# Odd modulation tiles scaled and accumulated by GpSimd, key reciprocals taken over 512 columns

## What is computed

```python
mod = c_act @ w_mod[l] + b_mod[l]                       # 2048 x 12288, one row of c
sh1, sc1, g1, sh2, sc2, g2 = split(mod, 6)
h = rms_norm(x, norm_attn[l]) * (1.0 + sc1) + sh1       # likewise with sc2, sh2 before the ffn
...
k = qk_norm_rope(concatenate([k_nope, k_rope], -1), k_norm_g, cos, sin)   # rmsnorm over 192
```

## Time and profile before

| | |
|---|---|
| three runs | 2112.49, 2118.07, 2120.44 us, median 2118.07 |
| the profiled execution | 2113.76 us, its span 2112.0 us |
| PE busy | 2075.8 us, 98% |
| DVE busy | 1577.2 us, 75% |
| ACT busy | 1008.3 us, 48% |
| POOL busy | 54.4 us, 3% |
| read from memory | 476 MB, 228 GB/s on average |

### The profile page before, as it was taken

The page is one execution under the profiler, slowest core; times in us unless marked ns, Lnnn a source line. Parts: engine busy times, 40 slices in busy tenths (PEclk is TensorE's granted clock), DMA queues, the critical chain, the costliest instruction groups (busy, mean ns, idle before and its releaser), DMA issues.

```text
span 2112.0 us, 41562 instructions
## 1 busy us (share of the span) xinstructions
PE 2075.8 (98%) x17878; PEld 2041.3 (97%) x17878; DVE 1577.2 (75%) x2034; ACT 1008.3 (48%) x1293; POOL 54.4 (3%) x87
## 2 busy tenths in 40 slices
PE   7999999999999999999999999999999999999999
PEld 7999999999999999989999888999999999999998
DVE  7998788688577888687877798676666666666666
ACT  5444343444445476564446555454444444444443
POOL 1000000000000000000002102000000000000000
PEclk9999999999999999999999999999999999999998
DMA  7897887789676687577796664456666666666663
GB/s 251 279 351 273 307 306 270 252 290 325 210 260 178 212 287 265 176 260 252 258 347 204 217 178 140 148 168 194 195 181 207 193 194 195 183 207 192 195 194 120
DMA packets 248430, 481.13 MB, mean 228 GB/s; under 512 B 28331, under 2 KB 57623, under 8 KB 248247
## 3 DMA queue, kind: packets, MB, share of 16 engines
q1 hardware_dynamic: 247487, 478.26, 69.7%
q0 software_dynamic: 528, 0.15, 0.0%
q10 hardware_dynamic: 232, 0.06, 0.0%
HBM read 476.27 MB, written 8.44 MB: 230 GB/s over the span
## 4 chain that ended last, share of the span: by engine, by line
PE 93%; DVE 3%; issue 1%; ACT 1%; DMA 1%; POOL 0%; SPq 0%; DVEq 0%; ACTq 0%
PE acc L1797 87%; PE side L1797 3%; PE sums L1797 2%; PE sums L2074 1%; DVE w_lo L1125 1%; DMA mod_raw<-in_w_mod 1%; DVE mod_acc L1113 1%; PE acc L1904 0%; ACT prob L978 0%; ACT w_hi L629 0%; DMA x_tok<-in_x 0%; DVE m_prob L1510 0%; DMA raw<-in_b_w_out 0%; POOL prob L609 0%; PE acc L2348 0%
## 5 line engine op out<-in xcount | busy, mean ns | idle before, releaser
L1125 DVE TENSOR_TENSOR w_lo<-raw,w_hi 128x1024 fp32r<-128x1024 f32 x679 | 831.0, 1232 | 428.2 <-ACT w_hi L629 427.2
L629 ACT ACTIVATE w_hi<-raw 128x1024 fp32r<-128x1024 f32 x679 | 716.8, 1060 | 845.3 <-PE acc L1797 758.5
L1797 PE MATMUL acc<-h_hi,w_hi 128*128 128x256 f32 x3728 | 885.3, 280 | 17.6 <-issue 11.8
L1797 PE MATMUL acc<-h_lo,w_hi 128*128 128x256 f32 x3728 | 876.0, 277 | 0.0
L1797 PEld LDWEIGHTS acc<-h_hi,w_hi 128*128 128x128 f32 x3728 | 703.3, 189 | 32.1 <-issue 23.4
L1797 PEld LDWEIGHTS acc<-h_lo,w_hi 128*128 128x128 f32 x3728 | 703.4, 189 | 0.3 <-issue 0.2
L1797 PE MATMUL acc<-h_hi,w_lo 128*128 128x256 f32 x3728 | 502.4, 277 | 0.0
L1797 PEld LDWEIGHTS acc<-h_hi,w_lo 128*128 128x128 f32 x3728 | 460.4, 188 | 0.0
L1113 DVE SCALAR_TENSOR_TENSOR mod_acc<-mod_raw,silu_c,mod_acc 128x1024 f32<-128x1024 f32 x180 | 230.9, 1283 | 11.2 <-DMA mod_raw<-in_w_mod 11.2
L1797 PE MATMUL acc<-f_hi,w_hi 128*128 128x256 f32 x704 | 164.3, 276 | 0.0
L1797 PE MATMUL acc<-f_lo,w_hi 128*128 128x256 f32 x704 | 164.1, 276 | 0.0
(11 more groups left out here) (320 smaller groups left out, 2041.8 us busy)
## 6 DMA issues: line engine op xcount, KB each, us to landing
mod_raw<-in_w_mod SPq DMA_DIRECT2D x192, 512.0 KB, 5.9
raw<-in_w_up SPq DMA_DIRECT2D x176, 512.0 KB, 4.4
raw<-in_a_w_in SPq DMA_DIRECT2D x128, 512.0 KB, 5.1
raw<-in_w_down SPq DMA_DIRECT2D x88, 512.0 KB, 4.4
raw<-in_a_w_out SPq DMA_DIRECT2D x64, 512.0 KB, 5.0
raw<-in_w_in SPq DMA_DIRECT2D x56, 512.0 KB, 4.1
raw<-in_b_w_in SPq DMA_DIRECT2D x40, 512.0 KB, 4.7
raw<-in_a_w_group SPq DMA_DIRECT2D x32, 512.0 KB, 5.4
```

The source lines that it names most:

```text
L629: last = act.activation(w_hi[s][:, :], raw[s][:, :], ACT.Copy)
L1125: last = dve.tensor_tensor(w_lo[s][:, :], raw[s][:, :], f32(w_hi[s][:, :]), ALU.subtract)
L1797: return pe.matmul(o, lhsT, rhs, start=start, stop=stop, skip_group_check=True)
```

## The change

- `mod_tiles` is written a second time for POOL: the odd tiles of the first five vectors (80 tiles) are scaled in place (`tensor_scalar`) and added into `mod_acc` (`tensor_tensor`), two instructions of 128x1024; DVE keeps the even ones and all of the sixth vector. `mod_used` becomes two semaphores. `MOD_PACE` runs from (306, 134) straight to (336, 160).
- The keys: PE multiplies ones by the squares themselves (512 columns, at the last slab of the gates), ACT takes the root over 512 columns, DVE the reciprocal over 512 columns. The four key columns on PE, `m_diag` and the copy are gone.
- The first slab behind a norm (`first_slab`) does high by high first, then low by high, then high by low, so that it starts with `h_hi` alone. DVE splits three of the slabs, and ACT two, inside the norm loop and not before it.
- DVE adds the two halves of the summed squares, so that `norm_sums` has two matmuls less.
- The products with `w_uk` and `w_uv` go to `sums` and `side` for their first halves; the second out-projection keeps two sets open over all eight slabs; `m_low(0, 2)` moves ahead of `m_soft` for the last pair; at the very end `turn_out(2)` moves into the last slab.

```diff
+GP_MODS = 5
-            (294, 128), (314, 148), (324, 148), (336, 160), (341, 160), (363, 176), (385, 186), (396, 192))
+            (294, 128), (306, 134), (336, 160), (341, 160), (363, 176), (385, 186), (396, 192))
                     if n >= MOD_RING:
-                        sp.wait_ge(mod_used, n + 1 - MOD_RING)
+                        sp.wait_ge(mod_used[(n - MOD_RING) % 2], (n - MOD_RING) // 2 + 1)
+            def mod_tiles(first, end):
+                for n in range(first + 1, end, 2):
+                    v, k = n // MOD_TILES, n % MOD_TILES // 2
+                    x, o = mod_raw[n % MOD_RING], mod_acc[:, 1024:2048]
+                    gp.wait_ge(mod_landed[n % MOD_RING], (n // MOD_RING + 1) * 16)
...
+                        gp.tensor_scalar(x[:, :], x[:, :], silu_c[:, k:k + 1], 1.0, ALU.mult, ALU.mult).then_inc(mod_scaled, 1)
+                        gp.wait_ge(mod_scaled, mod_steps.value())
+                        gp.wait_ge(mod_used[1], n // 2)
+                        gp.tensor_tensor(o, o, x[:, :], ALU.add).then_inc(mod_used[1], 1)
+            gp.wait_ge(csilu_ready, 1)
+            mod_tiles(0, 104)
             for m in range(1, 4):
                 gp.wait_ge(sq_ready, m + 1)
...
+            mod_tiles(104, GP_MODS * MOD_TILES)
-                act.wait_ge(m_recip, pairs.value())
-                for n in range(4):
-                    last = act.activation(m_diag[:, n * P:(n + 1) * P], tab("ident"), ACT.Copy, scale=m_rinv[:, n:n + 1])
-                last.then_inc(m_diag_ready, 1)
+            def m_key_roots():
+                act.wait_ge(m_spread, pairs.value())
+                act.activation(m_kroot[:, :], sums[:, 1, :], ACT.Sqrt, bias=eps_key[:, :]).then_inc(m_kroot_ready, 1)
+            def m_key_reciprocals():
+                dve.wait_ge(m_kroot_ready, pairs.value())
+                dve.reciprocal(m_kinv[:, :], m_kroot[:, :]).then_inc(m_kinv_ready, 1)
+                    if j % 2 and n < GP_MODS * MOD_TILES:
+                        continue
             def h_split(shift):
                 for j in range(KD // 2):
                     h_part(j, shift)
+                    if j < 2:
+                        split(1)
...
+            def first_slab(a, hi, lo, x_hi, x_lo, k, ready):
+                pe.wait_ge(h_hi_ready, ready + 1)
+                for x, (w, starts) in ((x_hi, (hi, True)), (x_hi, (lo, False)), (x_lo, (hi, False))):
...
+            def m_spreads(n):
+                if n:
+                    pe.wait_ge(m_turned_in, heads.value())
+                pe.wait_ge(m_folded, pairs.value())
+                mm(sums[:, 1, :], ones[:, 0:P], flat(tmp[0][:, 0:2, :]), start=True, stop=True).then_inc(m_spread, 1)
...
-            sets = [set_free()]
+            pe.wait_ge(att[0]["mix_hi"], TILES)
+            homes = [sums_tiles]
```

More of the change, by code:

```diff
@@ L1201, in norm @@
                     low(j)
+                    if j < 3:
+                        split(1)
                     if j + 2 < KD // 2:
@@ L1537, in _ @@
                 at, last = pair_at(n), n == PAIRS - 1
+                if last:
+                    m_low(0, 2)
                 if n:
@@ L1543, in _ @@
                     rope_keys()
-                if last:
-                    m_low(0, 2)
                 split_to(at + 7)
@@ L1823, in last_slab, with gemm @@
                         last.then_inc(tail_done, 1)
+                        if between:
+                            between()
                 last.then_inc(slab_used, 1)
                 slabs.step()
-            def gemm(n_slabs, x_hi, x_lo, tiles, k=SLAB_K, n=SLAB_N, before=None, x0=0, between=None, a=None, parts=None, tail=False):
+            def first_slab(a, hi, lo, x_hi, x_lo, k, ready):
+                pe.wait_ge(h_hi_ready, ready + 1)
+                for x, (w, starts) in ((x_hi, (hi, True)), (x_hi, (lo, False)), (x_lo, (hi, False))):
+                    if w is lo:
+                        pe.wait_ge(lo_ready, slabs.value(RING + 1))
+                    if x is x_lo:
+                        pe.wait_ge(h_lo_ready, ready + 1)
+                    for i in range(4):
+                        for kk in range(k):
+                            last = mm(a[:, i, :], w[:, kk, i * P:(i + 1) * P], x[:, kk, :], start=starts and i % 2 == 0 and kk == 0)
+                last.then_inc(slab_used, 1)
+                slabs.step()
+            def gemm(n_slabs, x_hi, x_lo, tiles, k=SLAB_K, n=SLAB_N, before=None, x0=0, between=None, a=None, parts=None, tail=False, first=None):
                 if a is None:
@@ L1834, in gemm @@
                     lo = w_lo[w][:, 0:k * n].rearrange("p (k n) -> p k n", k=k)
+                    if first is not None and s == 0:
+                        pe.wait_ge(hi_ready, slabs.value(1))
+                        first_slab(a, hi, lo, x_hi, x_lo, k, first)
+                        continue
                     if before:
@@ L1843, in gemm @@
                             x = s * k + kk + x0
-                            first = s == 0 and kk == 0 and i % 2 == 0
-                            mm(a[0:rows, i, :], hi[:, kk, c0:c0 + rows], x_hi[:, x, :], start=first)
+                            starts = s == 0 and kk == 0 and i % 2 == 0
+                            mm(a[0:rows, i, :], hi[:, kk, c0:c0 + rows], x_hi[:, x, :], start=starts)
                             mm(a[0:rows, i, :], hi[:, kk, c0:c0 + rows], x_lo[:, x, :])
@@ L1973, in _ @@
                 for m in range(2):
-                    gemm(8, h_hi, h_lo, four, before=h_ready(0))
+                    gemm(8, h_hi, h_lo, four, before=h_ready(0), first=0 if g == 0 and m == 0 else None)
                     if g == 0 and m == 0:
@@ L2263, in _ @@
             for m in range(3):
-                gemm(8, h_hi, h_lo, four, before=h_ready(24))
+                gemm(8, h_hi, h_lo, four, before=h_ready(24), first=24 if m == 0 else None)
             for m in range(2):
@@ L2284, in _ @@
                 slabs.step()
-            sets = [set_free()]
+            pe.wait_ge(idx_relu, TILES)
+            homes = [side]
             for r in range(2):
@@ L2325, in _, with ff_up @@
             ffs = Count()
-            def ff_up(before=None):
-                for m in range(2):
-                    gemm(8, h_hi, h_lo, four, before=before)
+            def ff_up(before=None, first=None):
+                gemm(8, h_hi, h_lo, four, before=before, first=first)
+                gemm(8, h_hi, h_lo, four, before=before)
             def ff_down(a):
```

204 lines of the change are left out of this document (101 added, 103 removed).

## The result

The changed kernel takes 2175.0 us, the median of four runs (2159.2 to 2191.0), against 2117.1 for the kernel before (2112.5 to 2120.4, four runs): a ratio of 1.027, 95% interval 1.023 to 1.031. It is slower, and outside the forecast range of 2095 to 2148. The profiled execution is one of 2191.0 us.

A forecast was written before the change was run, and what follows sets the result against it. PE, busy 98% of the span, was taken as the bound, DVE close behind. Losses of 32 us less gains of 24.6 made +7.4 on the profiled 2113.76, 2121; the runs' median being 4.3 higher, 2125, range 2095 to 2148.

The forecast's parts named there:

- The price of POOL's tiles: Odd modulation tiles on POOL: their turns slow DVE, PE waits; 26 of the 32 us of losses.
- The turns: A two-input SBUF instruction of DVE and a POOL instruction do not run side by side but take turns.
- The price of a tile: Each odd tile on POOL costs DVE 2.6 us against 1.2 saved, net 1.4; bounds of the cost 1.3 to 2.95.
- setting the net work of a stretch against its time: PE waits in a stretch only by what DVE's work exceeds its time and lead; 11 us in slabs 16 to 62.
- Key columns: Pairs: four key columns, eight matmul instructions, leave PE's path, 0.81 us for each of 8 pairs: 6.5 us gained.
- Start of the out-projection: PE's 3.51 us wait for m_low(0, 2) goes, and with it a clock dip worth 1.7: 5.2 us gained.
- Accumulator sets and norms: Waits for accumulator sets and xT go (3.3, 3.0, 1.2 us); the two norms gain 1.8.
- the fifth slab behind the norm: PE starts 2.8 us sooner, but the fifth slab's high part comes late, about 1052.0; 1.2 us of gain left.
- The end: Last chain: 8 token-square instructions go and 8 transposes move into the last slab; 2.5 us gained.
- The ports cost little: Rival, chance 0.32: POOL's instructions fall on DVE's waits, loss 6 us, gains of 24.6 stay; 2099 us.
- POOL is late and holds up SP: Rival, chance 0.26: SP waits for POOL's tile use, weight loads queue behind; 2147 us, or 2143 with part of it.
- P: DVE is blocked while POOL works; the forecast's losses from this were 32 us, between 6 and 54.

The follow-up runs named there:

- e1: The changed kernel without POOL's share, all modulation tiles back on DVE: 2135.4 us, ratio 1.001 to the kernel before.
- e6: e1 with the modulation tiles' pace of the kernel before: three runs at 2105.7 to 2113.5 us, seven at 2132 to 2141, ratio 1.004.
- e9: e6 with the norm ahead of the feed-forward part as in the kernel before: ratio 0.9945 to the kernel before.
- e3: The changed kernel with POOL's two instructions working in place on the accumulator's odd half, not the loaded tile: 2140.7, 2169.7, 2170.4, 2170.7 us.
- e5: e3 with SP's waits corrected so that SP no longer waits for POOL: 2139.7, 2141.0, 2164.4, 2167.5 us.

## Why the prediction was wrong, point by point

It gave 24.6 us of gains and 32 of losses, +7.4 on the profiled execution. Measured, with the wide spacing taken out: +44.6. Two terms failed, the price of POOL's tiles by 24 us and the gains by 14.

**The price of POOL's tiles, 26 forecast, 49.8 measured.** 26 is the sum of 32 less the 6 that I gave to the reciprocals and the denser pace. By stage, changed kernel against e1, from the start of ACT's high part of one slab to that of another, wide spacing taken out (the forecast's column holds those 6 too, in the last two rows):

| stage | forecast of the whole loss | measured, POOL's share |
|---|---|---|
| start to slab 66 | 11 | 10.7 |
| slabs 66 to 122 | 3 | 5.3 |
| slabs 122 to 192 | 1.5 | 2.9 |
| slabs 192 to 245 | 0 | 2.5 |
| pairs, slabs 245 to 289 | 5.5 | 19.3 |
| slab 289 to the in-projection | 11 | 9.0 |

*The turns* were read rightly from the earlier trace rows, and the Trainium skill's page "SBUF — State Buffer", section "Who interferes with whom", has them as the trace does: an instruction of DVE with two inputs in SBUF and one of POOL that reads SBUF exclude each other for a whole instruction. The trace agrees: the two `w_lo` shown above end 1.1 us after their additions. *The price of a tile was too high*: every DVE instruction of the changed kernel against the median of its form before adds up to 149 us too long, 6 of them in e1 too: 1.8 for each of the 80 odd tiles, not 2.6. With 1.28 saved the net is 0.5, and by DVE's busy time 46.7/80, 0.6, not 1.4. *The step that failed is the one after it*: setting the net work of a stretch against its time. With the measured 0.6 that sum gives 120.5 + 16 x 0.6 = 130.1 in slabs 16 to 62, which fits into 130.5, and yet 10.7 us were lost up to slab 66. That the forecast had 11 there is luck: a price too high made up for what the sum leaves out. In the pairs 13 us net and 17.5 of reciprocals against 150 gave 5.5; in slabs 134 to 188, 141.5 "fits into 147". Work comes in bursts: an addition of 2.4 us in front of a low part, then a tile, then the next low part. One such burst is longer than DVE's lead of 1.1, and PE, which is busy all the rest of the time, never makes a wait good. In the pairs the bursts also hit instructions that I hadn't put on the path:

```profile
847.61 2.39 POOL L617 TENSOR_TENSOR mod_acc<-mod_acc,mod_raw 128x1024 f32<-128x1024 f32 x1
847.71 2.83 DVE L1539 TENSOR_TENSOR m_prob<-m_prob,m_inv 128x512 f32<-128x512 f32 x1
850.60 0.88 PE L2123 MATMUL sums<-table,m_prob 128*128 128x128 f32 x6 [3.23 <-DVE m_prob L1539]
```

The scaling of the probabilities, 0.68 us when alone, took 2.83, and PE stood 3.23. *The clock was left out of the loss*, though I had counted it among the gains. Behind this wait comes a stretch at a granted clock of 0.50, and so it is behind some of the others, not all (none behind the 2.36 us until 116.20). There are 11 such stretches in the changed kernel and 6 in e1. At half speed they cost at most 31.0 and 18.4 us. By the pages PE is idle 70.9 us of the span against 38.5, so 32.4 of idle time and 12.6 of clock make 45.0 of the 49.8; the other 4.8 I can't place.

**The gains, 24.6 forecast, 5 measured in e1, 11 in e6.** The table's denser pace took 4 to 6 back, which the forecast had only as a part of its 32.

*Key columns, 6.5 forecast, 1.0 measured* (e6 against before, slabs 245 to 289). The term was right: where nothing waits, a pair takes 27.8 us (in e6, from PE's first matmul that reads `kq` at 760.2 to the next pair's at 788.0) where it took 28.6. But PE now waits for `kq L1520`, three times, 2.8 us, and for `m_prob` once. PE came sooner and DVE did not.

*Start of the out-projection, 5.2 forecast, nothing measured.* I named what would be late next, the key copy, and took it as gone without a number. It is exactly as late, 3.54 against 3.51. In the changed kernel PE waits 3.1 for `h_lo` and 2.2 for the key copy there.

*Accumulator sets and norms, 9.3 forecast.* The waits of the earlier trace rows for ACT are gone. From slab 289 to the feed-forward part e6 gained 10.2 us, and 1.6 of it are two pairs' key columns, so that this term was about right. So was the fifth slab behind the norm. Its high part was forecast 13.9 us after PE's start (1038.1 to 1052.0), it came after 13.7, and PE waited 1.2 us for it (against the earlier trace rows):

```profile
1093.59 1.20 PE L1835 MATMUL acc<-h_hi,w_hi 128*128 128x256 f32 x4
...
1107.33 1.04 ACT L656 ACTIVATE w_hi<-raw 128x1024 fp32r<-128x1024 f32 x1
```

*The end, 2.5 forecast.* The last sums take 2.69 instead of 4.61 and the transposes 1.72 instead of 3.53, but the turned-out pieces went into the last slab:

```profile
2177.72 2.69 PE side L1835 x24
2180.40 1.72 PE acc L2397 x8
```

The feed-forward part as a whole is 1.3 us shorter in e9 (734.1 against 735.4), so half of the term came.

**The rivals.** "The ports cost little" failed on 143 us of lengthened instructions. "POOL is late and holds up SP" gave 2143 to 2147, nearer to the result than the forecast, and its sign was right. But its mechanism is refuted: SP was held 52.6 us, as in e3 50.8, and e5 shows no cost of it. Its price had been borrowed from the upper end of P, so that it came nearer by luck. Its condition had a slip too: 26 tiles in 30 slabs of 2.72 us are 9.4 us for three, not 8.2.

**The spacing** had no place in the forecast. It moves half of the changed kernel's runs by 28 us, four times the forecast's own net.

## What to carry to other kernels

Before work is given to GpSimd beside a VectorE that lives on two-input instructions in SBUF, price GpSimd's instruction as a turn that VectorE waits out, and compare that turn with VectorE's lead at its tightest place, not with the stretch's mean load. When TensorE is the bound, its waits add to the time, and a dip of the clock behind them can come on top (32.4 and 12.6 us here). For each wait that an edit removes, work out the end time of what is late next; here it was as late in the out-projection and in the pairs, and some 10 us of forecast gains were not there.

## What the runs showed of the hardware

PE starts 128x256 matmuls in one of two rhythms, 113.3 or 117.7 ns apart, at the same granted clock of 1.00 and with no waits. In these traces a rhythm of such matmuls lasts until PE's stream is broken, and then it can change: in the changed kernel the wide one holds from the wait that ends at 1439.92 to the last slab, some 6,190 matmuls. It decides 28 of some 2110 us here, and the wide one came in 19 of 88 runs of the kernel before. Two medians of few runs of such a kernel can differ by 1% with nothing changed; the count of matmuls in a fixed stretch of the trace tells which rhythm a run had. What selects it was not found.

A VectorE instruction that meets a GpSimd addition is lengthened by most of the overlap: of the `w_lo` in the changed kernel that lay beside an addition alone, 47, the mean overlap was 1.69 us and the mean lengthening over the median of 1.22 was 1.48; beside a scaling alone, 60, they were 0.89 and 0.02, since there it was mostly GpSimd that waited (1.90 us at the mean for a scaling of 1.12).
